# A two-layer hybrid encoder on one core: another order at the start of a layer, other banks for attention's values, and the retention norm's sums from rounded halves

## The reference

```python
h = rms_norm(x, norm_mix_g[l])
aq, ak, av, rq, rk, rv, rg, sz, sxbc, sdt = jnp.split(h @ w_in[l], offs, axis=-1)
...
mu = jnp.mean(y, axis=-1, keepdims=True)
var = jnp.mean(jnp.square(y - mu), axis=-1, keepdims=True)
yn = ((y - mu) * lax.rsqrt(var + EPS)).reshape(Bn, S, R_WIDTH) * gn_g.astype(jnp.float32)
return (jax.nn.silu(g.astype(jnp.float32)) * yn).astype(v.dtype)
```

## Time and profile before

| | us |
|---|---|
| median of 3 runs | 1306.26 (1304.59 to 1306.29) |
| the profiled execution | 1307.44 |
| its span, first to last instruction | 1305.6 |
| TensorE busy | 1277.4 |
| VectorE, ScalarE, GpSimd busy | 615.3, 565.3, 588.8 |

### The profile page before, as it was taken

How to read it: one execution, slowest core, us unless ns; L and a number is a source line. 1 busy time by engine, 2 the same in 40 slices (tenths; PEclk the granted TensorE clock), 3 DMA queues, 4 the chain that set the end, 5 groups by cost and what they waited for, 6 DMA issues and landing times.

```text
span 1305.6 us, 21212 instructions
## 1 busy us (share of the span) xinstructions
PE 1277.4 (98%) x6114; PEld 1032.3 (79%) x6114; DVE 615.3 (47%) x938; ACT 565.3 (43%) x902; POOL 588.8 (45%) x435
## 2 busy tenths in 40 slices
PE   7999999999999999999999999999999999999996
PEld 4888877778888888888878887777888888888885
DVE  6755666474444103332256556755653430133323
ACT  6432483465444223443344327726644332244433
POOL 4533434254444544554444443424455454455541
PEclk9999999999999999999999999999999999999998
DMA  7335212143333333333323432212333333333333
GB/s 221 91 111 137 74 56 74 49 112 90 96 96 96 97 97 97 96 96 90 98 89 89 131 106 73 76 47 67 91 111 98 96 101 97 91 96 97 96 95 113
DMA packets 77483, 125.29 MB, mean 96 GB/s; under 512 B 7752, under 2 KB 20456, under 8 KB 77288
## 3 DMA queue, kind: packets, MB, share of 16 engines
q1 hardware_dynamic: 77416, 124.43, 33.6%
HBM read 121.84 MB, written 2.55 MB: 95 GB/s over the span
## 4 chain that ended last, share of the span: by engine, by line
PE 83%; DVE 8%; ACT 4%; issue 4%; DMA 0%; DVEq 0%; SPq 0%; ACTq 0%
PE dense L1048 76%; PE mix L1048 6%; DVE h_lo L690 1%; ACT w_hi L481 1%; DVE arena L991 1%; DVE ssq L698 1%; DVE arena L739 1%; ACT L525 1%; DVE arena L993 1%; ACT m_hi L498 0%; DMA x<-in_xT 0%; DVE arena L910 0%; ACT pad L525 0%; DVE mx L920 0%; DVE arena L926 0%
## 5 line engine op out<-in xcount | busy, mean ns | idle before, releaser
L378 POOL TENSOR_TENSOR w_lo<-w_raw,w_hi 128x512 fp32r<-128x512 f32 x424 | 580.3, 1384 | 686.8 <-ACT w_hi L481 680.1
L1048 PE MATMUL dense<-h_hi,w_hi 128*128 128x512 f32 x1120 | 445.3, 398 | 3.9 <-DVE h_lo L690 3.0
L1048 PE MATMUL dense<-h_lo,w_hi 128*128 128x512 f32 x1120 | 437.3, 390 | 0.0
L481 ACT ACTIVATE w_hi<-w_raw 128x512 fp32r<-128x512 f32 x422 | 256.3, 627 | 258.4 <-PE dense L1048 242.4
L1048 PE MATMUL dense<-h_hi,w_lo 128*128 128x512 f32 x1120 | 300.5, 389 | 0.0
L1048 PEld LDWEIGHTS dense<-h_hi,w_hi 128*128 128x128 f32 x1120 | 211.0, 188 | 55.3 <-issue 10.0
L1048 PEld LDWEIGHTS dense<-h_lo,w_hi 128*128 128x128 f32 x1120 | 211.0, 188 | 45.2 <-issue 2.7
L1048 PEld LDWEIGHTS dense<-h_hi,w_lo 128*128 128x128 f32 x1120 | 210.4, 188 | 44.4
L1048 PE MATMUL dense<-m_hi,w_hi 128*128 128x512 f32 x544 | 217.3, 400 | 3.2 <-ACT w_hi L481 2.5
L1048 PE MATMUL dense<-m_lo,w_hi 128*128 128x512 f32 x544 | 212.0, 390 | 0.0
L1048 PE MATMUL dense<-m_hi,w_lo 128*128 128x512 f32 x544 | 146.9, 389 | 0.0
(11 more groups left out here) (173 smaller groups left out, 958.3 us busy)
## 6 DMA issues: line engine op xcount, KB each, us to landing
w_raw<-in_w SPq DMA_DIRECT2D x428, 256.0 KB, 2.6
arena<-cum_rows SPq DMA_DIRECT2D x8, 512.0 KB, 5.7
x<-in_xT SPq DMA_DIRECT2D x8, 256.0 KB, 6.3
out_y<-arena SPq DMA_DIRECT2D x8, 256.0 KB, 2.1
arena<-exp_rows SPq DMA_DIRECT2D x12, 128.0 KB, 6.4
consts<-in_consts SPq DMA_DIRECT2D x1, 1223.0 KB, 9.2
rel_scratch<-arena SPq DMA_DIRECT2D x1, 382.0 KB
bias<-rel_scratch SPq DMA_DIRECT2D x8, 32.0 KB, 2.5
```

The costliest lines, as they stand in the source:

```text
L378: nc.gpsimd.tensor_tensor(w_lo[:, s, :], w_raw[:, s, :], w_hi[:, s, :].bitcast(f32), ALU.subtract).then_inc(lo_ready, 1)
L481: nc.scalar.activation(w_hi[:, slot, :], w_raw[:, slot, :], ACT.Copy).then_inc(hi_ready, 1)
L1048: return T.matmul(dst, lhsT, rhs, start=start, stop=stop)
```

## The change

It has four parts. First, the group's second half is issued in another order. `H0` and `H1` are the high and the low-by-high products of units 0 and 1 for packs 4 to 7, and stand ahead of `NORM` and `DT`; `L0` to `L3` end the units; VectorE's and ScalarE's `U0` to `U3`, `DX` (dt's evacuation), `CR` and `CX` (the evacuations of `CM`) stand elsewhere in the list, the convolutions run in the order of `CONV_ORDER`, and ScalarE rounds weights up to other packs. The dt weights are cleared and scaled by GpSimd and not by VectorE. Second, `NORM` uses bank 1. Third, `AV0` stays in bank 0, and `AV1` to `AV3` go to bank 5. Fourth, the retention norm: `RQ` squares all four tiles and rounds the squares into `m_hi`, VectorE subtracts to get `m_lo` (`RN` for two tiles, `RM` for the others), TensorE adds two rounded products against rounded ones, and ScalarE takes four logarithms, rounds two packs of weights, and takes four exponentials.

```diff
-    "G0 G1 G2 G3 NORM U0 DT U1 U2 TK U3 TT D4 DTB D5 DTC D6 D7 CM D8 BC TOL D9 SA0 D10 D11 SB0 SA1 D12 D13 SB1 SA2 D14 D15 "
+    "G0 G1 G2 G3 H0 H1 NORM DT L0 U0 DX L1 U1 L2 L3 TT TK D4 U2 DTB D5 D6 DTC U3 D7 CR CX D8 CM BC TOL D9 SA0 D10 D11 SB0 SA1 D12 D13 SB1 SA2 D14 D15 "
...
-    "RB0 RA1 D32 RB1 RA2 D33 RB2 RA3 D34 RB3 D35 RN0 D36 D37 RX0 D38 RX1 D39 RN1 D40 D41 RX2 D42 RX3 "
+    "RB0 RA1 D32 RB1 RA2 D33 RB2 RA3 D34 RB3 D35 RQ0 D36 RN0 D37 RM0 D38 RX0 D39 RX1 D40 RX2 D41 RX3 D42 "
...
-    "NORM": (5,), "DT": (5,), "TK": (4,), "CM": (4, 5), "BC": (0, 2, 3), "SA": (0,), "SB": (1, 4, 5),
-    "AS": (0, 1, 4), "AT": (2, 3), "AV": (0,), "RP": (4,), "RV": (5,), "SN": (4,),
-    "RA": (0, 1, 2), "RB": (3, 4, 5), "RN": (0, 1),
+    "NORM": (1,), "DT": (5,), "TK": (4,), "CM": (4, 5), "BC": (0, 2, 3), "SA": (0,), "SB": (1, 4, 5),
+    "AS": (0, 1, 4), "AT": (2, 3), "AV0": (0,), "AV": (5,), "RP": (4,), "RV": (5,), "SN": (4,),
+    "RA": (0, 1, 2), "RB": (3, 4, 5), "RN": (0, 1), "RM": (2, 3),
...
-        rs2 = (ssq, rstd)
+        rs4 = (ssq[:, :], rstd[:, :], sq[:, 0, :], sq[:, 1, :])
+        sq4 = (sq[:, 0, :], sq[:, 1, :], pad[:, 0, 4:4 + S], pad[:, 1, 4:4 + S])
+        ones_r = sb("ones_r", [P, P], f32r)
...
+            nc.gpsimd.memset(wdt_g[:, :, :], 0.0).then_inc(wdt_zero, 1)
+            pool.wait_ge(p_loaded, 16)
+            pool.wait_ge(wdt_loaded, 16)
+            pool.wait_ge(wdt_zero, 1)
             with pool.Fori(0, DEPTH) as l:
+                nc.gpsimd.tensor_tensor(wdt_g[:, :, 0:8],
...
                     elif step == "U":
                         if n:
-                            hi_to(2 * GROUP + SLOTS - 1)
-                        if n == GROUP - 1:
-                            hi_to(2 * GROUP + SLOTS + 1)
+                            hi_to({1: 11, 2: 13, 3: 19}[n])
...
-                    elif step == "RN":
-
-                        if n == 0:
-                            act.wait_ge(m_free[4], ready("RB3", 1, l) + 1)
-                            for j in range(2):
-                                nc.scalar.activation(sq[:, j, :], ry[:, j, :], ACT.Square).then_inc(r_sq, 1)
...
+                    elif step == "RQ":
+
+                        act.wait_ge(m_free[4], ready("RB3", 1, l) + 1)
+                        for t in range(4):
+                            nc.scalar.activation(sq4[t], ry[:, t, :], ACT.Square).then_inc(r_sq, 1)
+                        for t in range(4):
+                            act.wait_ge(r_sq, l * 4 + t + 1)
+                            nc.scalar.activation(m_hi[:, 8 + t, :], sq4[t], ACT.Copy).then_inc(r_sqh, 1)
+                    elif step == "RM":
+                        where = [("RN0", 0), ("RN0", 1), ("RM0", 0), ("RM0", 1)]
+                        for t, (name, i) in enumerate(where):
+                            act.wait_ge(m_ready[t], ready(name, i, l))
+                            nc.scalar.activation(rs4[t], M[t][:, :], ACT.Ln, scale=1.0 / P,
+                                                 bias=par["eps"][:, 0:1]).then_inc(m_free[t], 1)
+                        hi_to(packs[0] + 1)
+                        for t, (name, i) in enumerate(where):
+                            act.wait_ge(m_free[t], ready(name, i, l) + 1)
+                            nc.scalar.activation(rs4[t], rs4[t], ACT.Exp, scale=-0.5).then_inc(r_rs, 1)
...
             dve.wait_ge(c_loaded, 16 * N_CONST_LOADS)
+            link(V.tensor_copy(ones_r[:, :], ones[:, :]))
...
+                    elif step in ("RN", "RM"):
+                        for t in (0, 1) if step == "RN" else (2, 3):
+                            dve.wait_ge(r_sqh, l * 4 + t + 1)
+                            V.tensor_tensor(m_lo[:, 8 + t, :], sq4[t], m_hi[:, 8 + t, :].bitcast(f32), ALU.subtract).then_inc(r_sql, 1)
...
+                def group_high(u):
+
+                    for k in range(SLOTS, KD):
+                        h_tile(l * 2)(k)
+                        pe.wait_ge(hi_ready, l * N_PACKS + k + 1)
+                        group_mm(u, k, False)
+
+                def group_low(u):
+
+                    for k in range(SLOTS, KD):
+                        pe.wait_ge(lo_ready, l * N_PACKS + k + 1 + SLOTS)
+                        ins = group_mm(u, k, True, stop=k == KD - 1)
+                    ins.then_inc(run_done, 1)
+
+                def group_last(u):
+
+                    for k in range(SLOTS, KD):
+                        group_mm(u, k, False)
+                        group_mm(u, k, True, stop=k == KD - 1).then_inc(run_done, 1)
...
-                    elif step == "RN":
+                    elif step in ("RN", "RM"):
                         for j in range(2):
-                            pe.wait_ge(r_sq, l * 4 + 2 * n + j + 1)
+                            t = j if step == "RN" else 2 + j
+                            pe.wait_ge(r_sql, l * 4 + t + 1)
                             take(name, j, l)
-                            mm(M[j][:, :], ones[:, :], sq[:, j, :]).then_inc(m_ready[j], 1)
+                            mm(M[t][:, :], ones_r[:, :], m_hi[:, 8 + t, :], True, False)
+                            mm(M[t][:, :], ones_r[:, :], m_lo[:, 8 + t, :], False, True).then_inc(m_ready[t], 1)
```

More of the change, by code:

```diff
@@ L439, in rms @@
             def rms(e, name, l):
[L441 to L444, removed]
+                act.wait_ge(m_ready[1], ready(name, 0, l))
+                nc.scalar.activation(rstd[:, :], M[1][:, :], ACT.Ln, scale=1.0 / D,
+                                     bias=par["eps"][:, 0:1]).then_inc(m_free[1], 1)
+                act.wait_ge(m_free[1], ready(name, 0, l) + 1)
                 nc.scalar.activation(rstd[:, :], rstd[:, :], ACT.Exp, scale=-0.5).then_inc(rstd_ready, 1)
@@ L546, in _ @@
                         nc.scalar.activation(dt_u[:, :], dt_u[:, :], ACT.Ln).then_inc(dt_ln, 1)
-                    elif step == "CM":
-                        act.wait_ge(m_ready[5], ready(name, 1, l))
+                    elif step == "CR":
+                        hi_to(21)
+                        act.wait_ge(m_ready[5], ready("CM", 1, l))
                         nc.scalar.activation(crows[:, 0, :], M[5][:, 0:P], ACT.Copy).then_inc(rows_done, 1)
@@ L757, in _ @@
                         dve.wait_ge(run_done, l * N_SEGS + (SEG0 + UNIT_END[n]))
-                        row = pad[:, n % 2, 3:3 + S]
+                        row = pad[:, CONV_ORDER.index(n) % 2, 3:3 + S]
                         if n < 2:
@@ L804, in _ @@
                             V.tensor_tensor(xs[:, t, :], xs[:, t, :], row, ALU.mult).then_inc(yg_done, 1)
-                    elif step == "DT":
-                        dve.wait_ge(m_ready[5], ready(name, 0, l))
+                    elif step == "DX":
+                        dve.wait_ge(m_ready[5], ready("DT", 0, l))
                         V.tensor_tensor(dts, M[5][:, :], rstd[:, :], ALU.mult).then_inc(m_free[5], 1)
@@ L831, in _ @@
                                                ALU.mult, ALU.mult).then_inc(dt_done, 1)
[L832 to L833 removed]
+                    elif step == "CX":
+                        dve.wait_ge(m_ready[4], ready("CM", 0, l))
                         link(V.tensor_copy(tok[:, 32:64], M[4][:, 0:32]))
                         V.tensor_copy(lastb[:, :], M[4][:, 32:64]).then_inc(m_free[4], 1)
[L836 removed]
+                        dve.wait_ge(m_free[4], ready("CM", 0, l) + 1)
                         V.tensor_tensor(wdec[:, :], lastb[:, :], tok[:, 32:64], ALU.subtract).then_inc(wdec_in, 1)
@@ L1092, in norm @@
                 take(name, 0, l)
-                mm(M[5][:, :], ones[:, :], ssq[:, :]).then_inc(m_ready[5], 1)
+                mm(M[1][:, :], ones[:, :], ssq[:, :]).then_inc(m_ready[1], 1)
             def take(name, i, l):
-                pe.wait_ge(m_free[BANKS_OF(name)[i]], ready(name, i, l))
+                pe.wait_ge(m_free[banks_of(name)[i]], ready(name, i, l))
             with pe.Fori(0, DEPTH) as l:
@@ L1150, in _ @@
                         group_pack(n)
-                    elif step == "U":
-                        group_unit(n)
+                    elif step == "H":
+                        group_high(n)
+                    elif step == "L":
+                        if n == GROUP - 1:
+                            group_last(n)
+                        else:
+                            if n == GROUP - 2:
+                                group_high(n)
+                            group_low(n)
                     elif step == "D":
@@ L1160, in _ @@
                             elif n == N_IN + 8:
-                                pe.wait_ge(m_free[0], ready("AV3", 0, l) + 1)
+                                pe.wait_ge(m_free[5], ready("AV3", 0, l) + 1)
                             dense_unit(n, m_src(4 * part), ret_tile if n == N_IN + 16 else None)
```

82 lines of the change are left out of this document (32 added, 50 removed).

## The result

The changed kernel takes 1330.62 us (median of 4 runs, 1329.52 to 1331.6) against 1306.28 for the kernel before on the same chip: ratio 1.0186, 95% interval 1.0169 to 1.0204. It is 24.3 us slower; the forecast was 1 us slower, with a range that ended at 1312.

What follows compares the result with a forecast made beforehand. TensorE was taken to bound the kernel, busy 1277.4 of 1305.6 us. Terms -4.35 - 0.4 - 2.2 + 8.0 gave +1.0 us on the median 1306.26, so 1307.3, range 1302 to 1312.

Steps and rivals of the forecast that it cites:

- Start of a layer: Layer 0: H0 and H1 ahead of the norm cover its wait and avoid the low clock; gain 4.35 us, bounds 2.6 to 5.2.
- Pack 7: Start of layer 0: its rounding ends at 22.65, so H0 waits 0.9 us for it.
- D6's wait: Layer 1 start: VectorE evacuates D4 ahead of U2, so dense unit 6 no longer waits; gain 0.4 us.
- The price of this order: Layer start: VectorE's U0 convolution comes some 2 us later against TensorE in layer 1, covered by 21.8 us of units.
- Attention: AV2 in bank 5 starts 1.77 us sooner; 1.1 us kept per layer, 2.2 in all, bounds 0.5 and 1.77 each.
- Retention norm: RN0 and RM0 wait for low halves behind evacuations, then RX steps delay units; loss 4.0 us a layer, 8.0 in all.
- full clock: After the 0.9 us idle at the layer start the clock stays full, as it did behind an earlier wait of 1.84.
- D43 and D44: Dense units after the retention norm: they wait 1.1 and 1.15 us for evacuations behind four RX steps in a row.
- the lock with GpSimd: At RN0, VectorE's two-SBUF-input subtractions cannot run beside GpSimd's; low halves come at 248.05 and 249.7.

Runs made afterwards that it cites:

- start and banks, with cures: Changed kernel with the old retention norm, ScalarE taking CM's rows before D7's silu and rounding packs 22 and 23 before SA0's exponentials: 1298.65 us (ratio 0.9946).

## Why the prediction was wrong

**Start of a layer, right.** TensorE's rows after, against the earlier trace rows:

```profile
20.88 0.47 PE L1071 MATMUL dense<-h_hi,w_hi 128*128 128x512 f32 x1 [0.22 <-ACT w_hi L500]
24.15 1.12 PE L1071 MATMUL mix<-ssq,consts 128*128 128x512 f32 x2 [0.75 <-DVE ssq L718]
...
35.26 0.49 PE L1071 MATMUL dense<-h_hi,w_hi 128*128 128x512 f32 x1
```

D4 starts 5.2 us sooner than before (forecast 4.35, "near 36"), the granted clock is 1.00. Pack 7 was less late than I had it, 0.22 and not 0.9, so H0 and H1 ended near 23.2 and not at 25.02, and TensorE waited 0.75 for the sum of squares, which ended at 24.0, near the 24.2 of the forecast. The norm starts 0.9 sooner than forecast for it. The result holds some luck: the kernel before had 1.7 of the 5.2 us in its stretch at 0.50 behind the norm, and the profiles of two kernels with the same start, the one with the retention norm alone and the one with attention's banks alone, have no such stretch. Without it 3.5 are left, and with 0.3 for D6's wait, which is gone, and 2.6 for the banks this makes 6.4, where 6.5 were measured.

**The price of this order, wrong, and this is the step that failed:** "It is covered as long as it stays under the units in between: from D8's start to the first SSD product there are four units of 24 matmuls, 21.8 us." The rows came 5 us later against TensorE, not 2, and above all the cover was not measured. I counted TensorE's work up to the consumer that I had in mind, the SSD product, and set nothing against it: the chain from the rows (12.7 us to the rounding, by the rows of before at 68.10 and 80.79) and what stands behind it in ScalarE's queue. The first consumer is D11, whose start is one unit sooner, and its room was 0.3 and 0 us. I had read the waits, where a wait of 0 looks the same with no room and with much. The price: 11.0 us of waits and, with 11.0 us of work at half speed behind them, another 5.5.

**Attention, right.** AV2's wait went, 0.3 came back at AV3 and 0.4 at RP2 in each layer; forecast 2.2, measured 2.6 alone.

**Retention norm, right in mechanism and nearly in size at full clock.** TensorE's waits in layer 0:

```profile
250.76 0.50 PE L1071 MATMUL mix<-m_hi,ones_r 128*128 128x512 f32 x1 [2.24 <-DVE m_lo L1010]
...
252.44 0.79 PE L1071 MATMUL mix<-m_hi,ones_r 128*128 128x512 f32 x1 [0.95 <-DVE m_lo L1010]
...
258.68 0.49 PE L1071 MATMUL mix<-m_hi,ones_r 128*128 128x512 f32 x1 [1.46 <-DVE m_lo L1010]
...
274.59 0.50 PE L1071 MATMUL dense<-m_hi,w_hi 128*128 128x512 f32 x1 [0.79 <-DVE x L805]
...
278.39 0.50 PE L1071 MATMUL dense<-m_hi,w_hi 128*128 128x512 f32 x1 [0.78 <-DVE x L805]
```

Forecast were 2.4, 1.2, 1.6, and 1.1 and 1.15 for D43 and D44; the term was 8.0 us against 7.9. What the lock with GpSimd costs is seen on VectorE: in the changed kernel the pair took 3.15 us from 249.17 beside GpSimd, the next pair 1.28 without it. This agrees again with the lock of the Trainium skill (page SBUF — State Buffer, section Who interferes with whom). The sum failed here too in what it left out: the clock stood at 1.00 behind the single wait of 1.84 in the earlier trace rows, so I took full clock throughout, but RN0's are two waits within 2 us. They cost 1.4 + 2.9 us more in the changed kernel. The Trainium skill says of a long wait on DMA (page TensorE: Matmul & The Clock Gate, section HAM oscillation — how this bites in real kernels) that TensorE is throttled again across it, and that the next stretch of work starts slow. The windows behind D11's waits of 5.00 and 6.01 us agree, though these were ended by ScalarE. That 2.24 and 0.95 us close together do the same is shown only by the windows here.

The account: -6.5 (start and banks, with cures), +11.0 and +5.5 (D11 and its clock), +7.9 and +4.3 (norm and its clock) make 22.2 of the 24.3, whose interval is 22.1 to 26.6. The other 2.1 us have no name here; by the times D11 and its clock cost 1.3 more than these rows give.

## What to carry to other kernels

Before TensorE is moved ahead, measure the room of every consumer behind that place: the end of what it needs in the trace against its own start, not its wait, which is 0 either way. Engines that issue in order hide chains: weights for a dense unit can wait for a DMA that has nothing to do with them, and the cure is to move the two instructions that stand behind it. A long wait of TensorE, or two short ones close together, is to be priced with what the clock costs behind it: here 5.5 us behind 11.0 us of waits at D11.

## What was unexpected of the hardware

The low clock isn't the same from run to run at the same place. All eight waits of 4.7 to 7.0 us before D11 (in four kernels that keep the cause) had a stretch at 0.50 behind them, but its length was 6.8 us in seven and 3.4 in one. The three waits at RN0 and RM0 had one at eight of ten places, 3.4 or 6.8 us long. The first norm's wait was 3.36 us in the kernel before and is followed by 0.50; in the kernel with the retention norm alone it was 3.24 and in that with attention's banks alone 3.21, and the clock stayed at 1.00. What decides in such a case was not found: the waits themselves differ by 0.1 us. It is worth up to 3.4 us a place between one profile and another, half of what TensorE works in the stretch.
